# Where the Vector engine forms the quarter sums of the activations for the down projection

## The chip, the cores and the metric

The kernel runs on one core of a Trainium2 chip. The metric is the device time of one execution in microseconds (us); where several executions are compared, it is their median. TensorE (PE) multiplies matrices, VectorE (DVE) and ScalarE (ACT) work elementwise, GpSimd (POOL) helps, and SyncE (SP) issues most of the loads.

## What is computed

One layer of a decoder trunk, for a prompt of 512 tokens and 8 sample tokens, 520 in all. The change touches only its last part, the feed-forward block:

```python
    xn = rmsnorm(x, g2)
    up = xn @ w_up                                  # 1024 -> 2 * 2816
    pad = jnp.concatenate([conv_buf.astype(up.dtype), up], axis=1)
    conv = c_b + c_w[0] * pad[:, 0:S]
    for j in range(1, CONV_W):
        conv = conv + c_w[j] * pad[:, j:j + S]
    a, gval = jnp.split(conv, 2, axis=-1)
    x = x + (jax.nn.silu(a) * gval) @ w_down        # 2816 -> 1024
```

## The kernel before, in words

**Numbers in two parts.** Every f32 operand of a matmul is held as a high part in the reduced f32 format that TensorE takes (names in `h`, `whi`) and a low part, the rest (names in `l`, `wlo`). A product of two operands is three matmuls: high by high, high by low, low by high. ACT makes a high part by copying, DVE the low part by subtracting the high part from the original. Weights come by DMA into two buffers `raw_pair` (`raw[0]`, `raw[1]`), are split into `whi[0/1]` and `wlo[0/1]`, and slot n uses buffer n mod 2. A matmul takes 128 weight columns and 260 of the 520 tokens (`HALF`).

**Up projection.** It has 22 steps (`FT` = 22), i = 0 to 21, each of two tiles of 48 matmuls (t = 0 and 1). In step i DVE (`up_step`, L1629) scales a finished tile out of PSUM into `up[t]` (L1645), subtracts the low part of an earlier activation (`hidden_low`, L1622), makes `wlo` for the tile two slots on (`low`, L1083), runs the causal convolution (L1652 to L1656) and multiplies the two branches (L1660). The results are the activations `acth` (high) and `actl` (low), 22 blocks of 128 features by 520 tokens. Steps 1 to 17 are a hardware loop on DVE; steps 18 to 21 are written out.

**Down projection.** The 22 blocks of activations are cut into groups of 8, 7 and 7. There are 8 output tiles. For the first 6, taken as 3 pairs (`pairs_d`), the group of 8 blocks is done with a scheme of 7 products in place of 8 (`DownPair`, `down_pair`): a 2 by 2 block product, the quarters being 4 blocks by 260 tokens. It needs the activations' quarters as ordinary f32 sums and four combinations of them: with a quarter sum `acth + actl` called Q(k, h), k for the blocks (0 to 3 or 4 to 7) and h for the half of the tokens,

- act00 = Q(0,0), act01 = Q(0,1), act10 = Q(4,0), and dtf[1] = Q(4,1);
- combination 0 = act01 - act00, combination 2 = dtf[1] - combination 0, combination 1 = dtf[1] - act01, combination 3 = act10 - combination 2.

Each combination gets a high part `dth` (ACT) and a low part `dtl` (DVE, L1703). They are made once and serve all three pairs. Seven factors of each pair's weights are made likewise: DVE forms four sums `dsum` of weight blocks (L1709 to L1714), ACT their high parts, DVE their low parts (`factor_low`, L1491).

**The order around the change.** PE is one queue: after the last up tile it runs four slots of pair 0 (S_DN to S_DN + 3; 42 matmuls each, blocks 8 to 21), then products 0 to 6 of pair 0 (12 matmuls each), then pair 1, pair 2, a plain tile, and the last tile. A slot n begins when `w_lo` says that DVE's `low(n)` is done. Product f waits for `s_pl`, DVE's low part of factor f (`product`, L2175); product 3 waits besides for two low parts `dtl`, products 5 and 6 for the others (`s_tl`). DVE works in the order of its program too: three of the four quarter sums stand in steps 18, 19 and 20 (`extra=`, put between the two tiles of a step), the first combination in step 21; behind `hidden_low(21)` come, in this order, the fourth quarter sum, `low(S_DN+2)`, three subtractions that make the other combinations, `low(S_DN+3)`, four `dtl`, a memset, and pair 0's factors. ACT waits with `s_bt` for each combination in the order 0, 2, (high part of slot S_DN+3's weights), 1, 3, and only then makes the factors' high parts. SP issues the load into a raw buffer when the low part of its former contents is done.

Of the kernel before, what the change touches and what calls it, by code (L numbers as in the profile page):

```python
# [19 lines left out]
ALU = mybir.AluOpType  # L20
# [10 lines left out]
KT = D_MODEL // P  # L31
NC = SEQ // P
FT = D_FF // P
# [16 lines left out]
S_DN = S_UP + 2 * FT  # L50
# [36 lines left out]
def hybrid_layer(nc, ins, outs):  # L87
    with ExitStack() as ctx:
# [12 lines left out]
        def sem(name):  # L101
            return ctx.enter_context(nc.semaphore(name))
# [109 lines left out]
        def st(name, shape, offset):  # L212
            return nc.alloc_sbuf_tensor_at(name, shape, F32, offset=stage_at + offset)
# [20 lines left out]
        act00 = nc.alloc_sbuf_tensor_at("act00", [P, KT // 2, HALF], F32, offset=sp_at)  # L234
        act01 = nc.alloc_sbuf_tensor_at("act01", [P, KT // 2, HALF], F32, offset=ftmp_at)
        act10 = st("act10", [P, KT // 2, HALF], 0)
# [72 lines left out]
        def down_width(g):  # L309

            return (DN_CUTS[g + 1] - DN_CUTS[g]) * P
# [95 lines left out]
        s_bt = sem("x_combinations")  # L407
# [668 lines left out]
        def _(dve):  # L1076
            TT, TS, STT = dve.tensor_tensor, dve.tensor_scalar, dve.scalar_tensor_tensor

            def low(n, width=KT * P):

                p = n.c % 2
                dve.wait_ge(w_hi, n(1))
                TT(wlo[p][:, 0:width], raw[p][:, 0:width], whi[p][:, 0:width].bitcast(F32), ALU.subtract)\  # L1083
                    .then_inc(w_lo, 1)

            def ready(n):
                dve.wait_ge(done, n(2))

            def both(t):
                return t.rearrange("p (a b) -> p a b", a=2)  # L1090

            def out2(n):
                return out_ps[n.c % 2][:, :, 0:HALF]
# [525 lines left out]
            def hidden_low(i):  # L1619

                dve.wait_ge(s_ah, i + 1)
                TT(actl[:, i, :], silu[:, :], acth[:, i, :].bitcast(F32), ALU.subtract).then_inc(s_al, 1)  # L1622

            def quarter_sum(out, k0, h):

                part = (slice(None), slice(k0, k0 + KT // 2), slice(h * HALF, (h + 1) * HALF))
                TT(out, acth[part].bitcast(F32), actl[part].bitcast(F32), ALU.add)

            def up_step(i, first=False, last=False, extra=None):  # L1629
                for t in range(2):  # L1630
                    n = At(S_UP + t, i, 2)
                    f = i * 2 + t
                    if extra is not None and t == 1:
                        extra()
                    if first and t == 0:
                        dve.memset(up[0][:, 0:2], 0.0)
                        dve.memset(up[1][:, 0:2], 0.0)
                        dve.wait_ge(s_std2, 1)
                        dve.reciprocal(rbc2[:, :], rbc2[:, :])
                        low(n.plus(2))  # L1640
                        dve.drain()
                    ready(n)
                    if not first:
                        dve.wait_ge(s_nc, i * 2 + (t - 1))
                    TT(both(up[t][:, 2:2 + TOK]), out2(n), both(rbc2[:, :]), ALU.mult).then_inc(evac[n.c % 2], 1)  # L1645
                    dve.drain()  # L1646
                    dve.nop().then_inc(s_up, 1)
                    if t == 0 and not first:
                        hidden_low(i - 1)
                    if not (first and t == 0):  # L1650
                        low(n.plus(2), down_width(1 + t) if last else KT * P)
                    STT(conv[t][:, SEQ:TOK], up[t][:, 2 + SEQ:2 + TOK], cwb[:, f, 2:3], sconv[:, f, :], ALU.mult, ALU.add)  # L1652
                    dve.wait_ge(s_tap, i * 2 + (t + 1))
                    STT(conv[t][:, 0:SEQ], up[t][:, 1:1 + SEQ], cwb[:, f, 1:2], conv[t][:, 0:SEQ], ALU.mult, ALU.add)
                    dve.drain()
                    STT(conv[t][:, 0:SEQ], up[t][:, 0:SEQ], cwb[:, f, 0:1], conv[t][:, 0:SEQ], ALU.mult, ALU.add)\  # L1656
                        .then_inc(s_cv, 1)
                dve.drain()
                dve.wait_ge(s_sil, i + 1)
                TT(silu[:, :], silu[:, :], conv[1][:, :], ALU.mult).then_inc(s_pr, 1)  # L1660

            dve.wait_ge(s_scv, 1)
            up_step(0, True)
            with dve.Fori(1, FT - 4) as i:
                up_step(i)

            def first_difference():

                TT(act00[:, :, :], act01[:, :, :], act00[:, :, :], ALU.subtract).then_inc(s_bt, 1)

            up_step(FT - 4, extra=lambda: quarter_sum(act00[:, :, :], 0, 0))
            up_step(FT - 3, extra=lambda: quarter_sum(act01[:, :, :], 0, 1))
            up_step(FT - 2, extra=lambda: quarter_sum(act10[:, :, :], KT // 2, 0))
            up_step(FT - 1, last=True, extra=first_difference)
            hidden_low(FT - 1)

            def low_last():
# [78 lines left out]
                result()  # L1756

            dve.wait_ge(s_nc, 2 * FT)
            quarter_sum(dtf[:, 1, :, :], KT // 2, 1)
            low(At(S_DN + 2), down_width(1))  # L1760
            dve.drain()
            TT(dtf[:, 2, :, :], dtf[:, 1, :, :], act00[:, :, :], ALU.subtract).then_inc(s_bt, 1)
            TT(dtf[:, 1, :, :], dtf[:, 1, :, :], act01[:, :, :], ALU.subtract).then_inc(s_bt, 1)
# [685 lines left out]
```

## Time and profile before

| | us |
|---|---|
| median of 3 runs | 898.91 (898.21 to 899.29) |
| the profiled execution's own time | 898.24 |
| its span, first to last instruction | 896.4 |
| PE busy in the span | 887.7 (99%) |
| DVE busy | 609.7 (68%) |
| ACT busy | 390.5 (44%) |
| POOL busy | 133.0 (15%) |

The mean granted TensorE clock of the span is 0.997 of full speed. Busy shares are means over stages that differ. The last up tile ends near 765 us and pair 0 of the down projection lies between 765 and 795 us of the span; all times in the rows below are counted from the span's start. PE's rows overlap: the modelled duration of one matmul is 0.28 us, while one starts every 0.12 us, so the starts are what tells its pace. On DVE, too, an instruction may start a little before the row of the one ahead of it ends.

### The profile page before, as it was taken

What the parts mean: (1) busy time and instruction counts of PE and PEld (TensorE: products, weight loads), DVE (VectorE), ACT (ScalarE), POOL (GpSimd) and SP (SyncE); (2) the same over time, 40 slices, a digit from 0 to 9 for tenths busy, and PEclk for the clock granted to TensorE, in tenths of its full rate; (3) what the DMA queues carried; (4) which work ended last, traced back from release to release, by engine and by line L of the source; (5) the groups of instructions that cost most, each with busy time, mean ns of one, the idle gap of its engine ahead of it and who ended that gap; (6) DMA issues with size and microseconds to landing.
All of it is one profiled execution on the core that took longest, in us unless ns stands there. A gap on an engine that the chain in (4) does not pass through costs nothing.

```text
span 896.4 us, 18963 instructions
## 1 busy us (share of the span) xinstructions
PE 887.7 (99%) x7306; PEld 883.2 (99%) x7306; DVE 609.7 (68%) x980; ACT 390.5 (44%) x629; POOL 133.0 (15%) x182
## 2 busy tenths in 40 slices
PE   9999999999999999999999999999999999999997
PEld 8999999999999999999999999999999999999997
DVE  7895775442885568677755777777777778966544
ACT  7535434544864334344432344444444444433334
POOL 0673000002542110000005700000000000000001
PEclk9999999999999999999999999999999999999998
DMA  6332253234872222322255222222222222333232
GB/s 214 114 123 94 72 202 99 78 99 155 280 269 72 71 72 75 115 95 94 95 200 136 83 82 94 94 94 94 94 88 82 87 94 88 99 107 88 89 106 96
DMA packets 31499, 100.44 MB, mean 112 GB/s; under 512 B 4668, under 2 KB 7260, under 8 KB 31192
## 3 DMA queue, kind: packets, MB, share of 16 engines
q1 hardware_dynamic: 29256, 92.96, 31.2%
q0 software_dynamic: 1472, 5.72, 2.2%
q10 hardware_dynamic: 720, 1.04, 0.4%
q8 instruction: 36, 0.59, 0.3%
q14 instruction: 15, 0.12, 0.0%
HBM read 92.37 MB, written 7.35 MB: 111 GB/s over the span
## 4 chain that ended last, share of the span: by engine, by line
PE 88%; issue 3%; POOLq 3%; DMA 2%; DVE 2%; POOL 1%; ACT 0%; DVEq 0%; SPq 0%; ACTq 0%
PE out L1961 81%; PE trp L1961 3%; PE aux L1961 2%; POOLq L1939 2%; POOLq L1937 1%; DMA raw_pair<-in_w_slots 1%; PE trp L1995 1%; DMA cwb<-in_conv_wb 1%; PE aux L2153 0%; DVE wlo L1083 0%; DVE tf L1425 0%; DVE tl L1430 0%; POOL y L1952 0%; DVE tf L1421 0%; POOL out_conv_old L1923 0%
## 5 line engine op out<-in xcount | busy, mean ns | idle before, releaser
L581 ACT ACTIVATE whi<-raw_pair 128x1024 fp32r<-128x1024 f32 (+4 forms) x168 | 154.2, 924 | 210.3 <-PE out L1961 196.4
L1083 DVE TENSOR_TENSOR wlo<-raw_pair,whi 128x1024 fp32r<-128x1024 f32 (+1 forms) x121 | 154.0, 1273 | 89.6 <-ACT whi L581 89.2
L1961 PE MATMUL out<-xh,whi 128*128 128x260 f32 x668 | 143.4, 289 | 0.4 <-DVE wlo L1491 0.4
L1961 PE MATMUL out<-x2h,wlo 128*128 128x260 f32 x704 | 141.9, 283 | 0.0
L1961 PE MATMUL out<-x2h,whi 128*128 128x260 f32 x704 | 141.8, 282 | 0.0
L1961 PE MATMUL out<-x2l,whi 128*128 128x260 f32 x704 | 141.7, 283 | 0.0
L1961 PE MATMUL out<-xl,whi 128*128 128x260 f32 x668 | 139.3, 283 | 0.0
L1961 PE MATMUL out<-xh,wlo 128*128 128x260 f32 x668 | 139.2, 283 | 0.0
L1961 PEld LDWEIGHTS out<-x2h,whi 128*128 128x128 f32 x704 | 108.6, 188 | 0.1
L1961 PEld LDWEIGHTS out<-x2h,wlo 128*128 128x128 f32 x704 | 108.5, 188 | 0.0
L1961 PEld LDWEIGHTS out<-x2l,whi 128*128 128x128 f32 x704 | 108.2, 188 | 0.0
L1961 PEld LDWEIGHTS out<-xh,whi 128*128 128x128 f32 x668 | 105.4, 189 | 1.0 <-issue 0.6
L1961 PEld LDWEIGHTS out<-xh,wlo 128*128 128x128 f32 x668 | 105.0, 188 | 0.0
L1961 PEld LDWEIGHTS out<-xl,whi 128*128 128x128 f32 x668 | 104.9, 188 | 0.0
L1961 PE MATMUL out<-acth,whi 128*128 128x260 f32 (+2 forms) x266 | 58.2, 283 | 0.0
L1961 PE MATMUL out<-acth,wlo 128*128 128x260 f32 (+2 forms) x266 | 58.0, 283 | 0.0
L1961 PE MATMUL out<-actl,whi 128*128 128x260 f32 (+2 forms) x266 | 57.9, 283 | 0.0
L1645 DVE TENSOR_TENSOR up<-out,rbc 128x520 f32<-128x520 f32 x44 | 30.8, 701 | 38.9 <-PE out L1961 38.8
L1945 POOL COPY nconv<-up 128x10 f32 x44 | 10.4, 236 | 241.4 <-DVEq L1646 241.4
L581 ACT ACTIVATE acth<-silu 128x520 f32 (+1 forms) x22 | 14.1, 639 | 69.8 <-DVE silu L1660 69.8
L1961 PEld LDWEIGHTS out<-acth,whi 128*128 128x128 f32 x266 | 42.8, 188 | 0.1
L1961 PEld LDWEIGHTS out<-acth,wlo 128*128 128x128 f32 x266 | 42.8, 188 | 0.0
(362 smaller groups left out, 1755.8 us busy)
## 6 DMA issues: line engine op xcount, KB each, us to landing
raw_pair<-in_w_slots SPq DMA_DIRECT2D x123, 512.0 KB, 3.3
raw_pair<-in_w_dn SPq DMA_DIRECT2D x16, 448.0 KB, 3.4
c_ring<-in_C_state SPq DMA_DIRECT2D x8, 512.0 KB, 5.4
row<-scratch SPq DMA_DIRECT2D x8, 512.0 KB, 5.7
out_C_sample<-c_ring SPq DMA_DIRECT2D x8, 512.0 KB, 4.9
raw_pair<-in_w_dn SPq DMA_DIRECT2D x8, 512.0 KB, 3.5
xres<-in_x_all POOLq DMA_DIRECT2D x1, 1560.0 KB, 6.9
x<-in_x_all SPq DMA_DIRECT2D x5, 260.0 KB, 6.8
```

Of the source, the lines that this page charges most:

```text
L581: return act.activation(out, in_, func, **kw_)
L1083: TT(wlo[p][:, 0:width], raw[p][:, 0:width], whi[p][:, 0:width].bitcast(F32), ALU.subtract)\
L1645: TT(both(up[t][:, 2:2 + TOK]), out2(n), both(rbc2[:, :]), ALU.mult).then_inc(evac[n.c % 2], 1)
L1937: pool.drain()
L1939: pool.drain()
L1945: pool.tensor_copy(nconv[:, i * 2 + t, :], up[t][:, SEQ:2 + TOK]).then_inc(s_nc, 1)
L1961: return pe.matmul(*a, **k)
L1995: m = pe.transpose(trp[b.c % 2][:, c, :], ftmp[b.c % 2][:, c * P:(c + 1) * P], ident[:, :])
```

## The change

The three quarter sums in steps 18, 19 and 20 and the first combination in step 21 are taken out of the up projection. All four sums and all four combinations now stand behind `hidden_low(21)`. The steps 18 to 20 join the hardware loop. ACT, PE, SP and POOL keep their programs instruction for instruction; DVE runs the same operations on the same operands, four of them later.

```diff
             up_step(0, True)
-            with dve.Fori(1, FT - 4) as i:
+            with dve.Fori(1, FT - 1) as i:
                 up_step(i)
-
-            def first_difference():
-
-                TT(act00[:, :, :], act01[:, :, :], act00[:, :, :], ALU.subtract).then_inc(s_bt, 1)
-
-            up_step(FT - 4, extra=lambda: quarter_sum(act00[:, :, :], 0, 0))
-            up_step(FT - 3, extra=lambda: quarter_sum(act01[:, :, :], 0, 1))
-            up_step(FT - 2, extra=lambda: quarter_sum(act10[:, :, :], KT // 2, 0))
-            up_step(FT - 1, last=True, extra=first_difference)
+            up_step(FT - 1, last=True)
             hidden_low(FT - 1)
...
             dve.wait_ge(s_nc, 2 * FT)
+            quarter_sum(act00[:, :, :], 0, 0)
+            low(At(S_DN + 2), down_width(1))
+            quarter_sum(act01[:, :, :], 0, 1)
             quarter_sum(dtf[:, 1, :, :], KT // 2, 1)
-            low(At(S_DN + 2), down_width(1))
+            dve.drain()
+            TT(act00[:, :, :], act01[:, :, :], act00[:, :, :], ALU.subtract).then_inc(s_bt, 1)
+            quarter_sum(act10[:, :, :], KT // 2, 0)
             dve.drain()
             TT(dtf[:, 2, :, :], dtf[:, 1, :, :], act00[:, :, :], ALU.subtract).then_inc(s_bt, 1)
             TT(dtf[:, 1, :, :], dtf[:, 1, :, :], act01[:, :, :], ALU.subtract).then_inc(s_bt, 1)
```

In the rows below L1627 is the line of a quarter sum, L1083 that of `low`, and the number behind a name counts its buffer. On DVE, in step 21, between the convolution of the first tile and the scaling of the second, the row with the minus goes (one like it, an L1627, goes from each of steps 18 to 20):

```order
 L1654 SCALAR_TENSOR_TENSOR conv_84<-up_82,cwb,conv_84 128x512
 L1656 SCALAR_TENSOR_TENSOR conv_84<-up_82,cwb,conv_84 128x512
-L1669 TENSOR_TENSOR act_152<-act_153,act_152 128x1040
 L1645 TENSOR_TENSOR up_83<-out,rbc_87 128x520
 L1083 TENSOR_TENSOR wlo_123<-raw_pair,whi_121 128x896
```

The step's second tile now follows its first with nothing between them.

On DVE behind the last up step, before the change, from `hidden_low(21)` to the first `dtl`; `wlo1_124` is the low part of slot S_DN+2's weights, `wlo0_123` that of slot S_DN+3's:

```order
L1622 TENSOR_TENSOR actl_64<-silu_86,acth_119 128x520
L1627 TENSOR_TENSOR dtf_91<-acth_119,actl_64 128x1040
L1083 TENSOR_TENSOR wlo1_124<-raw_pair_120,whi1_122 128x896
L1762 TENSOR_TENSOR dtf_91<-dtf_91,act00_152 128x1040
L1763 TENSOR_TENSOR dtf_91<-dtf_91,act01_153 128x1040
L1765 TENSOR_TENSOR dtf_91<-act10_154,dtf_91 128x1040
L1083 TENSOR_TENSOR wlo0_123<-raw_pair_120,whi0_121 128x896
L1703 TENSOR_TENSOR dtl_90<-act00_152,dth_89 128x1040
```

The same place after the change (line numbers behind L1661 are 8 lower at first, 3 lower behind the edit):

```order
L1622 TENSOR_TENSOR actl_64<-silu_86,acth_119 128x520
L1627 TENSOR_TENSOR act00_152<-acth_119,actl_64 128x1040
L1083 TENSOR_TENSOR wlo1_124<-raw_pair_120,whi1_122 128x896
L1627 TENSOR_TENSOR act01_153<-acth_119,actl_64 128x1040
L1627 TENSOR_TENSOR dtf_91<-acth_119,actl_64 128x1040
L1756 TENSOR_TENSOR act00_152<-act01_153,act00_152 128x1040
L1627 TENSOR_TENSOR act10_154<-acth_119,actl_64 128x1040
L1759 TENSOR_TENSOR dtf_91<-dtf_91,act00_152 128x1040
L1760 TENSOR_TENSOR dtf_91<-dtf_91,act01_153 128x1040
L1762 TENSOR_TENSOR dtf_91<-act10_154,dtf_91 128x1040
L1083 TENSOR_TENSOR wlo0_123<-raw_pair_120,whi0_121 128x896
L1695 TENSOR_TENSOR dtl_90<-act00_152,dth_89 128x1040
```

`low(S_DN+2)` still has one instruction between it and `hidden_low`; between it and `low(S_DN+3)` there are seven in place of three.

## Rows read from the trace of the kernel before

**Rows 1.** The page, busy time and share of the span by engine.

```profile
PE 887.7 (99%) x7306; PEld 883.2 (99%) x7306; DVE 609.7 (68%) x980; ACT 390.5 (44%) x629; POOL 133.0 (15%) x182
```

**Rows 2.** Timeline, DVE, steps 17 to 19: start, duration, what, [idle before].

```profile
713.19 0.70 DVE L1645 TENSOR_TENSOR up<-out,rbc 128x520 f32<-128x520 f32 x1 [0.95 <-PE out L1961]
...
724.63 0.70 DVE L1645 TENSOR_TENSOR up<-out,rbc 128x520 f32<-128x520 f32 x1 [0.87 <-PE out L1961]
...
728.85 1.23 DVE L1627 TENSOR_TENSOR act<-acth,actl 128x1040 f32<-128x1040 f32 x1
730.40 0.70 DVE L1645 TENSOR_TENSOR up<-out,rbc 128x520 f32<-128x520 f32 x1 [0.32 <-PE out L1961]
...
736.16 0.70 DVE L1645 TENSOR_TENSOR up<-out,rbc 128x520 f32<-128x520 f32 x1 [1.03 <-PE out L1961]
```

**Rows 3.** Timeline, DVE, step 21 between its two tiles.

```profile
763.31 1.24 DVE L1669 TENSOR_TENSOR act<-act,act 128x1040 f32<-128x1040 f32 x1
765.00 0.70 DVE L1645 TENSOR_TENSOR up<-out,rbc 128x520 f32<-128x520 f32 x1 [0.45 <-PE out L1961]
```

**Rows 4.** Timeline, DVE, behind the last up step.

```profile
770.32 0.70 DVE L1622 TENSOR_TENSOR actl<-silu,acth 128x520 fp32r<-128x520 f32 x1 [0.76 <-ACT acth L581]
770.93 1.23 DVE L1627 TENSOR_TENSOR dtf<-acth,actl 128x1040 f32<-128x1040 f32 x1
772.09 1.08 DVE L1083 TENSOR_TENSOR wlo<-raw_pair,whi 128x896 fp32r<-128x896 f32 x1
773.26 1.24 DVE L1762 TENSOR_TENSOR dtf<-dtf,act 128x1040 f32<-128x1040 f32 x1
774.42 1.24 DVE L1763 TENSOR_TENSOR dtf<-dtf,act 128x1040 f32<-128x1040 f32 x1
775.75 1.24 DVE L1765 TENSOR_TENSOR dtf<-act,dtf 128x1040 f32<-128x1040 f32 x1
776.91 1.08 DVE L1083 TENSOR_TENSOR wlo<-raw_pair,whi 128x896 fp32r<-128x896 f32 x1
777.91 1.23 DVE L1703 TENSOR_TENSOR dtl<-act,dth 128x1040 fp32r<-128x1040 f32 x1
...
783.07 1.22 DVE L1491 TENSOR_TENSOR wlo<-raw_pair,whi 128x512 fp32r<-128x512 f32 x2
784.21 0.68 DVE L1709 TENSOR_TENSOR dsum<-raw_pair 128x512 f32<-128x512 f32 x1
...
787.16 2.52 DVE L1491 TENSOR_TENSOR wlo<-dsum,whi 128x512 fp32r<-128x512 f32 x4
```

**Rows 5.** Timeline, PE: starts of slot S_DN+3, product 0, product 1, product 2.

```profile
779.94 0.40 PE L1961 MATMUL out<-acth,whi 128*128 128x260 f32 x2
...
784.99 0.28 PE L1961 MATMUL trp<-acth,whi 128*128 128x260 f32 x1
...
786.41 0.28 PE L1961 MATMUL out<-acth,whi 128*128 128x260 f32 x1
...
787.73 0.28 PE L1961 MATMUL out<-acth,wlo 128*128 128x260 f32 x1
787.91 0.39 PE L1961 MATMUL out<-acth,whi 128*128 128x260 f32 x1
```

**Rows 6.** Timeline, ACT: combinations' high parts and slot S_DN+3's.

```profile
771.03 1.07 ACT L581 ACTIVATE dth<-act 128x1040 fp32r<-128x1040 f32 x1
774.54 1.08 ACT L581 ACTIVATE dth<-dtf 128x1040 fp32r<-128x1040 f32 x1 [2.44 <-DVE dtf L1762]
775.52 0.94 ACT L581 ACTIVATE whi<-raw_pair 128x896 fp32r<-128x896 f32 x1
776.36 2.02 ACT L581 ACTIVATE dth<-dtf 128x1040 fp32r<-128x1040 f32 x2
```

**Rows 7.** L471, the loads into the raw buffers, 740 to 800 us.

```profile
DMA to landing us min/median/max: 3.3/3.4/3.6
```

**Rows 8.** Waits of PE, 730 to 896 us: us in total, times, longest.

```profile
PE out L1961 <- ACT sqa L581: 0.6, 1, 0.6
PE aux L1961 <- DVE nd L1818: 0.6, 1, 0.6
```

**Rows 9.** Windows, PE, in the tail: us, busy (x), granted clock, DMA share, GB/s.

```profile
888.50:889.00 0.50, 0.01 (x1) 1.00 1.00 349
...
891.00:891.50 0.50, 0.41 (x4) 1.00 1.05 374
891.50:892.00 0.50, 0.00 (x0) 0.87 0.13 40
```

## The prediction

> **What bounds the kernel now.** I read the page's first part first: PE is busy 99% of the span and DVE 68% [rows 1]. That says only that PE must be kept fed; it doesn't say whether moving four DVE instructions is free. For that I took the two places between which they move, first on DVE's timeline, then on PE's.
>
> In the up projection PE sets the pace. The first tile of a step is scaled at 713.19, 724.63 and 736.16 us; the interval from step 18 (with a quarter sum) to step 19 is 11.53 us, and steps 17 to 18 (no sum) took 11.44, the loop's last step included. Each time DVE had waited for PE: 0.95 us in a step without a sum, and still 0.32 us right behind the quarter sum of 1.23 us [rows 2]. In step 21 the subtraction of 1.24 us is followed by 0.45 us of waiting [rows 3]. So before the change the four instructions lie wholly in time in which DVE would have waited.
>
> Behind the last up step it is the other way round. From 770.32 to 788 us DVE has no idle time in its rows but drains of a tenth [rows 4]. PE starts product 2 of pair 0 at 787.91, 0.18 us after the matmul ahead of it where the pace is 0.12; product 2 needs the low part of factor 2, the first of the four at 787.16, which ends near 787.16 + 0.69 = 787.85 [rows 4, 5]. So PE is already fed just in time there: DVE's chain has at most about 0.06 us to spare. From then until the last matmuls of the kernel PE waits for nobody: 0.6 and 0.6 us are all its waits of 730 to 896 us, both at the end, on the last squares and the last reciprocal [rows 8]. A delay at product 2 therefore has nowhere to vanish.
>
> **What is removed.** Steps 18 to 21 lose 1.23 or 1.24 us of DVE each. What comes next in each step is the scaling of a tile that PE has to finish first, so DVE's idle time there grows from 0.32 (0.45) to about 1.5 us and nothing starts earlier. Cost and gain 0. The steps 18 to 20 now run as loop passes; in the trace a looped and a written-out step both keep PE's interval, so 0 again.
>
> **What is added behind the last step.** DVE's start-to-start intervals: an instruction of 128x1040 with no drain behind it takes 770.93 to 772.09 = 1.16 us, and 773.26 to 774.42 = 1.16; `low` takes 776.91 to 777.91 = 1.00 us; with a drain behind it `low` takes 772.09 to 773.26 = 1.17 and the subtraction 774.42 to 775.75 = 1.33, so a drain costs 0.17 [rows 4]. Three quarter sums and one subtraction are added, and one drain: 4 x 1.16 + 0.17 = **4.81 us**. (The three new sums read the same operands in the same form as the old one, so its row prices them; bounds are 4 x 1.16 = 4.64 with a free drain and 4 x 1.24 + 0.17 = 5.13 without overlap.)
>
> The Trainium skill, in "VectorE: DVE Perf Modes", section "The DRAIN you can't avoid", says that the next operation doesn't issue until the pipeline is empty, whether or not a semaphore stands between. Taken literally that gives the upper of those bounds; the rows, with starts 1.16 us apart for a duration of 1.23, speak for the lower price.
>
> The new schedule, from 770.93: sum 00; `low(S_DN+2)` at 772.09, as before, so slot S_DN+2 is untouched; sum 01 at 773.09; sum 11 at 774.25; the first combination 775.58 to 776.82; sum 10 at 776.74; combinations 2, 1, 3 at 778.07, 779.23, 780.56; `low(S_DN+3)` at 781.72 in place of 776.91, ended 782.80.
>
> **What PE does with it.** Three waits open one after another, and together they make up the shift of DVE's chain:
> - Slot S_DN+3 started at 779.94 [rows 5]. It now waits for `low(S_DN+3)`, ended 782.80; with 0.06 us of signal it starts at 782.86: 2.92 us late.
> - It ran 779.94 to 784.99 = 5.05 us [rows 5], so it would end at 787.91. The factors' low parts come at 783.07 + 4.81 = 787.88; the first is done after half of 1.22 and a little overlap, 788.51. Product 0 starts at 788.57: 3.58 late, 0.66 more.
> - Products 0 and 1 take 787.91 - 784.99 = 2.92 us with the old gap, 2.86 without. Product 1's factor is done at 789.1, in time. Product 2 needs factor 2 at 787.85 + 4.81 = 792.66 and would be ready at 791.43: it starts at 792.72, 4.81 late in all, 1.23 more.
>
> Behind that DVE waited for ACT and PE before the change and waits again; the combinations' low parts are ready by 787.9, product 3 begins 1.5 us after product 2. So the shift stays 4.81.
>
> **Who else is shifted.** ACT waits with `s_bt` for the first combination: it ran at 771.03 and now starts at 776.86. Behind it in ACT's queue stand the second `dth` (DVE gives it at 779.31; 779.35 to 780.4) and the high part of slot S_DN+3's weights, which started 0.98 us after it [rows 6]: 780.33 to 781.27. DVE wants that at 781.72, so it is covered, by 0.45 us; were ACT late by more, `low(S_DN+3)` would move one for one. The two other `dth` end near 783.3 and DVE takes their low parts in its order 0, 2, 1, 3 from 782.72, the third at 785.0: covered. Two factors' high parts follow by 784.4, wanted at 787.88. SP's load for pair 0's second raw buffer waits for `low(S_DN+3)`: issued at 782.9, landed 3.4 us later [rows 7], 786.3; its first reader, the weight sum of 784.21, now comes at 789.0 [rows 4]. Covered by 2.7 us. SP's following loads wait for the weight sums and move with DVE, keeping their margins.
>
> **The forecast.** The profiled execution took 898.24 us (span 896.4), which gives 898.24 + 4.81 = 903.05. The median of the runs is 0.67 above that execution, and the sum moves with it: 898.91 + 4.81 = 903.72. I take 903.7, 0.5% slower; about 0.2% (1.8 us) is what a measurement of this kernel can tell from no change.
>
> **Rivals.**
> - **Only the first wait counts** (901.8). If the waits at products 0 and 2 had more slack than the rows say, PE would lose 2.92 us only. Against it: the gap of 0.18 us at 787.91 and the factor's end at 787.85 [rows 4, 5]. Chance 5%.
> - **The clock falls in the new wait.** The granted clock stayed 1.00 through half a microsecond with PE at 0.01, and fell to 0.87 in the window at 891.5, after about 3 us of thin work in the tail [rows 9]. A stall of 2.92 us is near that. If the clock were at its lower level, 1.2 GHz in place of 2.4, for all of slot S_DN+3, that slot would take 5.05 us more; but 0.66 + 1.23 = 1.89 us of it would fall into waits that exist anyway. That leaves 3.2 us: 906.9. Half such a spell costs 0.6 us. Chance of any such fall 12%; only half of that costs over 1.8 us.
> - **A pause at DVE's loop end.** The loop ends at step 20 now, next to the exposed stretch. In the trace the loop's end at step 17 leaves 0.87 us of waiting for PE [rows 2], so any pause there is hidden. The Trainium skill, "Runtime: NRT & Kernel Launch", section "Instruction fetch mechanics", says a taken branch whose target lies outside the fetched blocks stalls the engine for a transfer. As a mechanism here: a pause as long as a load's landing, 3.4 us [rows 7], less the 0.87 to 1.5 us in which DVE waits, lets PE run dry or moves the chain by some 2.2 us: 905.9. Chance 4%.
> - **The other side: the up projection gets faster** (not slower in all). The removed sums read and write SBUF beside PE's operands. If they had held PE up, steps 18 to 21 would shorten, and from 1.2 us a step on (4.81 / 4) the change would not lose. But a step with a sum takes 11.53 us and one without 11.44: at most 0.09 a step, 0.4 in all, 903.3. That the sum decides otherwise has 3%, and the same bucket holds any slack I have overlooked downstream.
>
> **How the numbers follow.** Forecast 76%, first wait only 5%, clock 12%, loop end 4%, other side 3%. The forecast itself reaches from 4.64 to 5.13, with half a microsecond either way for the medians: 903.0 to 904.6. To hold 8 in 10 against the rivals, the range goes from the first-wait case, 901.8, to 905.6, short of the full clock case. Faster by over 0.2% gets 2%, within 0.2% gets 3% (the other side and slack overlooked), slower 95%.
>
> **What would show it.** Right: in steps 18 to 21 DVE waits about 1.5 us before the second tile's scaling and PE's interval stays 11.53; `low(S_DN+3)` starts 9.6 us behind `low(S_DN+2)` in place of 4.8; PE shows waits on `wlo` L1083 of 2.6 to 2.9 us and twice on L1491, of 0.7 and 1.2, with the granted clock at 1.00; everything behind 793 us is 4.8 later. Wrong: shorter up steps, no wait at product 2, a clock below 1.00 near 783, or an ACT wait in front of `low(S_DN+3)`.

## The result, and the profile after

The changed kernel takes 903.50 us (median of 5 runs, 902.65 to 904.09), the kernel before 898.91 (5 runs, 898.21 to 899.29): a ratio of 1.0055, 95% interval 1.0043 to 1.0066, and the medians differ by 4.6 us where 4.8 was forecast. The profiled execution took 902.65 us with a span of 900.8 (898.24 and 896.4 before).

The page says almost nothing of it: PE's busy share is the same 99% [rows 1].

```profile
PE 889.7 (99%) x7306; PEld 884.9 (98%) x7306; DVE 611.1 (68%) x980; ACT 390.6 (43%) x629; POOL 130.7 (15%) x182
```

PE's waits over the whole span say more (engine, line, whom it waited for: us in total, times, longest). Two of its rows are new where the kernel before had no wait between 730 us and the tail [rows 8]:

```profile
PE out L1958 <- DVE wlo L1083: 2.7, 1, 2.7
...
PE out L1958 <- DVE wlo L1491: 0.2, 1, 0.2
```

DVE's timeline of the changed kernel, at steps 15 and 19 to 21 first (answering [rows 2, 3]), then behind the last step (answering [rows 4]). L1756 is the first combination:

```profile
689.80 0.70 DVE L1645 TENSOR_TENSOR up<-out,rbc 128x520 f32<-128x520 f32 x1 [0.95 <-PE out L1958]
...
741.61 0.70 DVE L1645 TENSOR_TENSOR up<-out,rbc 128x520 f32<-128x520 f32 x1 [1.15 <-PE out L1958]
...
747.46 0.70 DVE L1645 TENSOR_TENSOR up<-out,rbc 128x520 f32<-128x520 f32 x1 [0.96 <-PE out L1958]
...
753.14 0.70 DVE L1645 TENSOR_TENSOR up<-out,rbc 128x520 f32<-128x520 f32 x1 [1.15 <-PE out L1958]
...
758.91 0.70 DVE L1645 TENSOR_TENSOR up<-out,rbc 128x520 f32<-128x520 f32 x1 [0.87 <-PE out L1958]
...
764.67 0.70 DVE L1645 TENSOR_TENSOR up<-out,rbc 128x520 f32<-128x520 f32 x1 [1.60 <-PE out L1958]
...
771.76 1.08 DVE L1083 TENSOR_TENSOR wlo<-raw_pair,whi 128x896 fp32r<-128x896 f32 x1
772.76 1.23 DVE L1627 TENSOR_TENSOR act<-acth,actl 128x1040 f32<-128x1040 f32 x1
773.92 1.23 DVE L1627 TENSOR_TENSOR dtf<-acth,actl 128x1040 f32<-128x1040 f32 x1
775.23 1.24 DVE L1756 TENSOR_TENSOR act<-act,act 128x1040 f32<-128x1040 f32 x1
776.38 1.23 DVE L1627 TENSOR_TENSOR act<-acth,actl 128x1040 f32<-128x1040 f32 x1
...
781.34 1.08 DVE L1083 TENSOR_TENSOR wlo<-raw_pair,whi 128x896 fp32r<-128x896 f32 x1
```

Step 21's scaling now waits 1.60 us for PE where it waited 0.45, and starts no earlier in the step: 764.67 - 758.91 = 5.76 us behind the first tile's, 5.77 before (765.00 - 759.23). The steps 18 to 20, now loop passes, keep PE's interval too: from second tile to second tile 741.61, 753.14 and 764.67, so 11.53 us, as before from 730.40 to 765.00, three steps [rows 2, 3]. The two `low` start 9.58 us apart (4.82 before).

PE's timeline at the same place, answering [rows 5]; the last three rows are the start of product 0, the last matmul of product 1 and the start of product 2:

```profile
779.38 0.40 PE L1958 MATMUL out<-acth,wlo 128*128 128x260 f32 x2
782.48 0.50 PE L1958 MATMUL out<-acth,whi 128*128 128x260 f32 x2 [2.70 <-DVE wlo L1083]
782.83 0.51 PE L1958 MATMUL out<-actl,whi 128*128 128x260 f32 x2
783.13 0.64 PE L1958 MATMUL out<-acth,wlo 128*128 128x260 f32 x2
...
789.12 0.29 PE L1958 MATMUL trp<-acth,whi 128*128 128x260 f32 x1
...
791.89 0.28 PE L1958 MATMUL out<-acth,wlo 128*128 128x260 f32 x1
792.34 0.39 PE L1958 MATMUL out<-acth,whi 128*128 128x260 f32 x1 [0.17 <-DVE wlo L1491]
```

and the granted clock there (window, us, busy (x), granted clock as a share of 2.4 GHz, DMA share, GB/s):

```profile
782.00:783.00 1.00, 0.52 (x4) 0.98 0.00 0
783.00:784.00 1.00, 1.00 (x7) 0.50 0.62 98
784.00:785.00 1.00, 1.00 (x6) 0.50 0.89 344
785.00:786.00 1.00, 1.00 (x7) 0.50 0.21 82
786.00:787.00 1.00, 1.00 (x9) 0.82 0.00 0
787.00:788.00 1.00, 1.00 (x11) 1.00 0.00 0
```

Two things are seen. Product 2 starts 792.34 - 771.76 = 20.58 us behind `low(S_DN+2)`, 787.91 - 772.09 = 15.82 before: 4.76 us later. And the clock did fall: for about 3.4 us behind the wait it stood at its lower level of 1.2 GHz, and slot S_DN+3 took 789.12 - 782.48 = 6.64 us in place of 5.05. That rival had been given 12%, yet the time is that of the forecast. The experiments had to tell whether the 4.6 us are DVE's chain, with the clock's 1.59 us hidden, or the first wait and the clock together, 2.9 + 1.6, which gives nearly the same sum.

Counting from `low(S_DN+2)` is needed because executions differ by some tenths of a microsecond (once by 1.3) in what lies ahead: in the changed kernel's profile that instruction starts 0.33 us earlier than in the one before. The edited steps did not bring that: step 15, ahead of all that was edited, is already 0.32 us earlier (689.80 in the changed kernel). Its row in the kernel before:

```profile
690.12 0.70 DVE L1645 TENSOR_TENSOR up<-out,rbc 128x520 f32<-128x520 f32 x1 [0.95 <-PE out L1961]
```

4.76 - 0.33 = 4.43, and the two spans differ by 4.4.

### The profile page after: what moved, and what is told of

It reads as the page before. It is cut to its first block, busy times and chain, and to the rows that moved or that the text cites. A ratio compares the mean times of both kernels' runs of the same rounds, so it can differ in the third digit from the quotient of the medians.

```text
span 900.8 us, 19015 instructions
## 1 busy us (share of the span) xinstructions
PE 889.7 (99%) x7306; PEld 884.9 (98%) x7306; DVE 611.1 (68%) x980; ACT 390.6 (43%) x629; POOL 130.7 (15%) x182
## 4 chain that ended last, share of the span: by engine, by line
PE 88%; POOLq 3%; issue 3%; DVE 2%; DMA 1%; POOL 1%; ACT 1%; DVEq 1%; SPq 0%; ACTq 0%
PE out L1958 81%; PE trp L1958 3%; PE aux L1958 2%; POOLq L1936 2%; POOLq L1934 1%; PE trp L1992 1%; DMA cwb<-in_conv_wb 1%; DMA raw_pair<-in_w_slots 0%; DVE dtl L1695 0%; PE aux L2150 0%; POOL y L1949 0%; DVE act L1627 0%; DVE wlo L1083 0%; ACT whi L581 0%; POOL out_conv_old L1920 0%
## 5 line engine op out<-in xcount | busy, mean ns | idle before, releaser
L1083 DVE TENSOR_TENSOR wlo<-raw_pair,whi 128x1024 fp32r<-128x1024 f32 (+1 forms) x121 | 156.3, 1292 | 87.4 <-ACT whi L581 87.0
```

## Experiments

Times are medians; each group of kernels ran with the kernel before on its own chip (898.84 us for the first four, 898.20 for the next four, 898.55 for the last two). Beside its runs above, the changed kernel ran in the first group only. "Chain" is the theory that product 2 of pair 0 is late by as much as DVE's chain is longer.

**One, two and three late.** The first takes one instruction out of the up steps, the second two, the third three of the four:

```diff
-            up_step(FT - 2, extra=lambda: quarter_sum(act10[:, :, :], KT // 2, 0))
+            up_step(FT - 2)
...
             low(At(S_DN + 2), down_width(1))
+            quarter_sum(act10[:, :, :], KT // 2, 0)
             dve.drain()
```

> The kernel before, with one of the four moved instructions: the sum act10 is taken out of step 20 and stands behind low(S_DN+2). Theory of the chain (every late instruction delays product 2 of pair 0 by its start-to-start interval, 1.16 us, less 0.05 of slack): 1.1 us slower than before, near 900.0, PE waiting 1.1 us at product 2 and nowhere else, granted clock 1.00. Theory of the first wait and the clock (the loss is slot S_DN+3's wait, which has 1.95 us of slack in the kernel before, plus what the half-speed clock behind it takes): no change, 898.9.

> The kernel before, with two of the four moved: the sum act10 and the first combination act01 - act00 stand behind low(S_DN+2). Chain: 2 x 1.16 - 0.05 = 2.3 us slower, near 901.2, a wait of 0.4 us at slot S_DN+3 and 1.9 in all before product 2, clock 1.00. First wait and clock: 0.4 us slower, 899.3.

> The changed kernel with one sum left where it was: act00 in step 18; the sums act01 and act10 and the first combination are late, steps 18 to 20 written out. Chain: 3 x 1.16 + 0.17 - 0.05 = 3.6 us slower than before, near 902.5, slot S_DN+3 waiting about 1.7 us, too short for the clock to fall. First wait and clock: 1.7 us slower, 900.6.

> The changed kernel as it is, beside the three partial ones on the same chip. Both theories are built on it: 4.6 to 4.8 us slower than before, near 903.6. If the loss were not additive, the four kernels would not stand 1.1 to 1.3 us apart from each other.

Measured, with the places read from the four traces (the times of `low(S_DN+2)` and product 2 are starts in each kernel's own trace):

| late | median us | ratio to before, 95% | `low(S_DN+2)` | product 2 | between | more than before |
|---|---|---|---|---|---|---|
| 0 (before) | 898.84 | | 772.09 | 787.91 | 15.82 | |
| 1 | 899.18 | 1.0009 (1.0000 to 1.0018) | 771.65 | 788.60 | 16.95 | 1.13 |
| 2 | 901.21 | 1.0027 (1.0017 to 1.0037) | 772.50 | 790.60 | 18.10 | 2.28 |
| 3 | 902.46 | 1.0042 (1.0029 to 1.0056) | 771.52 | 790.94 | 19.42 | 3.60 |
| 4 (changed kernel again) | 903.61 | 1.0062 (1.0048 to 1.0076) | 771.88 | 792.46 | 20.58 | 4.76 |

The traces give a straight line: 1.13, 1.15, 1.32 (the one with the drain) and 1.16 us for the four. The theory of first wait and clock wanted 0, 0.4, 1.7 and 4.6; the medians of two (2.4 us) and three (3.6 us) late are far from its 0.4 and 1.7. For one late the median difference of 0.3 us alone can't decide; its interval (0 to 1.6 us) holds both. The spans of all executions, from first to last instruction, tell them apart better: their medians are 896.6 us before and 897.3, 898.9, 900.0 and 901.3 with one to four late, so 0.7, 2.3, 3.4 and 4.7 more. All 11 spans with one late are 897.0 us or longer, 16 of the 19 before are shorter, and the trace shows the new wait of 0.99 us at product 2. So one late does cost time. In the profiled executions the 0.7 us of span (897.1 against 896.4) are the 1.13 less the 0.44 by which `low(S_DN+2)` came earlier; the others have no trace. With two late, PE's three waits of the prediction stand side by side for the first time, with the clock at 1.00 throughout:

```profile
PE out L1963 <- DVE wlo L1491: 1.0, 1, 1.0
PE trp L1963 <- DVE wlo L1491: 0.4, 1, 0.4
PE out L1963 <- DVE wlo L1083: 0.2, 1, 0.2
```

A wait in these rows begins at the modelled end of the last matmul. By starts, one matmul every 0.12 us, each is 0.16 to 0.3 longer. Three late, where the first is 1.55 us, also left the clock alone:

```profile
781.08 0.51 PE L1960 MATMUL out<-acth,whi 128*128 128x260 f32 x2 [1.55 <-DVE wlo L1083]
...
786.78 0.39 PE L1960 MATMUL trp<-acth,whi 128*128 128x260 f32 x1 [0.39 <-DVE wlo L1491]
...
790.94 0.39 PE L1960 MATMUL out<-acth,whi 128*128 128x260 f32 x1 [1.02 <-DVE wlo L1491]
```

Here slot S_DN+3 at full clock would end at 781.08 + 5.05 = 786.13, and product 0 starts at 786.78: 0.65 late (the prediction had 0.66). Product 2 is 790.94 - 786.78 - 2.86 = 1.30 late (1.23).

**PE kept busy in the wait.** 22 matmuls whose result nobody reads:

```diff
                 for s in range(4):
                     t, g = s // 2, 1 + s % 2
                     if g == 1:
                         pe.wait_ge(evac[banks[t]], At(S_DN + pr.j + t).half(1))
+                    if pr.i == 0 and s == 3:
+                        for _ in range(22):
+                            MM(pr.p1, acth[:, 0, 0:P], acth[:, 0, 0:HALF], start=True, stop=True)
                     down_slot(...)
```

> The changed kernel, with 22 matmuls of 128x260 that nobody reads put on PE between slots S_DN+2 and S_DN+3 of pair 0, inside the wait of 2.7 us; they write the bank that product 0 overwrites. They should keep the granted clock at 1.00. Chain: the half-speed spell costs nothing, because PE waits at product 2 for DVE anyway; time unchanged at 903.5, and the 1.7 us that slot S_DN+3 gains turn into waits at products 0 and 2 (0.7 and 1.2 us, as the prediction had them). Clock: 1.7 us faster than the changed kernel, 901.8.

903.31 us, ratio 1.0056 (1.0042 to 1.0070). The clock stays up, here in the windows that had 0.50 in the changed kernel:

```profile
783.00:784.00 1.00, 1.00 (x11) 1.00 0.77 106
784.00:785.00 1.00, 1.00 (x11) 1.00 0.91 369
785.00:786.00 1.00, 1.00 (x10) 1.00 0.20 66
```

and what it gains comes back as waits, while product 2 starts as late as ever (792.19 - 771.61 = 20.58 us behind `low(S_DN+2)`, to the hundredth that of the changed kernel):

```profile
788.03 0.39 PE L1958 MATMUL trp<-acth,whi 128*128 128x260 f32 x1 [0.39 <-DVE wlo L1491]
...
792.19 0.39 PE L1958 MATMUL out<-acth,whi 128*128 128x260 f32 x1 [1.00 <-DVE wlo L1491]
```

So the fall of the clock costs nothing in the changed kernel: it takes 1.59 us, and 0.65 + 1.30 = 1.95 us of waiting stood behind it. The remainder, 0.36 us, is seen as the late start of product 2 behind product 1 in the changed kernel's trace (789.12 + 2.86 = 791.98 to 792.34).

**The sums done twice.** The steps stay as in the kernel before, and all four instructions are done again behind the last step (the edit is shown against the kernel before):

```diff
             def first_difference():
 
-                TT(act00[:, :, :], act01[:, :, :], act00[:, :, :], ALU.subtract).then_inc(s_bt, 1)
+                TT(act00[:, :, :], act01[:, :, :], act00[:, :, :], ALU.subtract)
...
             dve.wait_ge(s_nc, 2 * FT)
+            quarter_sum(act00[:, :, :], 0, 0)
+            low(At(S_DN + 2), down_width(1))
+            quarter_sum(act01[:, :, :], 0, 1)
             quarter_sum(dtf[:, 1, :, :], KT // 2, 1)
...
```

> The kernel before with its three sums and the first combination in steps 18 to 21 as they were, steps written out, and all of them done a second time behind the last step, in the order of the changed kernel. Chain: what stands in the up projection costs nothing and removing it earned nothing, so the same time as the changed kernel, 903.5, within 0.2. If the removal had earned something in steps 18 to 21 (0.09 us a step at most by the rows), or the loop's end had cost something, this kernel would differ from the changed one: up to 0.4 slower by the first, faster by the second.

903.30 us, ratio 1.0059 (1.0045 to 1.0072); product 2 at 792.39 - 771.81 = 20.58 us, the same as in the changed kernel. The two other kernels of its group in which DVE's way to product 2 is as long (below and above) take 903.42 and 903.31. The removal from the up steps earned nothing that can be seen, and loop or written-out steps make no difference.

**Slot S_DN+3 first.** On ACT the high part of that slot's weights goes ahead of the first combination's, on DVE its low part directly behind the first combination:

```diff
             TT(act00[:, :, :], act01[:, :, :], act00[:, :, :], ALU.subtract).then_inc(s_bt, 1)
+            low(At(S_DN + 3), down_width(2))
             quarter_sum(act10[:, :, :], KT // 2, 0)
...
-            low(At(S_DN + 3), down_width(2))
             down_combination_low(0, act00[:, :, :], 1)
```

> The changed kernel, but slot S_DN+3's weights are served early: ACT makes their high part before the first combination's, DVE their low part right behind the first combination, four instructions earlier. Nothing is added or left out. Chain: slot S_DN+3 starts on time, but product 2 is as late as in the changed kernel, the waits before products 0 and 2 add up to the same 4.7 us; 903.5, or up to 1.6 more if the longer wait before product 0 (3.6 us) lets the clock fall while products 0 and 1 run and only 1.2 us of that is hidden. First wait: the loss goes with the wait, 899 to 900.

903.42 us, ratio 1.0057 (1.0043 to 1.0070). The wait of 2.7 us is gone and the time is the same. Most of the debt now stands before product 0, which starts 788.41 - 771.99 = 16.42 us behind `low(S_DN+2)`, 784.99 - 772.09 = 12.90 in the kernel before, so 3.52 us later:

```profile
784.63 0.41 PE L1958 MATMUL out<-acth,wlo 128*128 128x260 f32 x2
788.41 0.39 PE L1958 MATMUL trp<-acth,whi 128*128 128x260 f32 x1 [3.36 <-DVE wlo L1491]
...
789.60 0.42 PE L1958 MATMUL trp<-acth,whi 128*128 128x260 f32 x1
789.82 0.42 PE L1958 MATMUL trp<-actl,whi 128*128 128x260 f32 x1
...
794.36 0.28 PE L1958 MATMUL trp<-dth,whi 128*128 128x260 f32 x1
```

The clock fell here too, 1.1 us after the wait, when products 0 and 1 ran (a start every 0.22 us from 789.60 to 792.85). That slowness fills the 1.24 us that are left before product 2, and a little more. Product 3 starts 794.36 - 771.99 = 22.37 us behind `low(S_DN+2)`, 793.87 - 771.76 = 22.11 in the changed kernel: 0.26 us is what was not hidden. It's too little to be seen in the medians.

**In the order in which PE needs it.** Everything stays late, but the four `dtl` (4.6 us on the path to product 2) move behind the factors 0 to 3, each ahead of the product that reads it, and slot S_DN+3's weights are served early. In short (ACT's high parts, not shown, follow the same order: slot S_DN+3's behind the first combination's, those of combinations 1 and 3 behind the factors 0 and 1):

```diff
             TT(act00[:, :, :], act01[:, :, :], act00[:, :, :], ALU.subtract).then_inc(s_bt, 1)
+            low(At(S_DN + 3), down_width(2))
             quarter_sum(act10[:, :, :], KT // 2, 0)
...
-            low(At(S_DN + 3), down_width(2))
-            down_combination_low(0, act00[:, :, :], 1)
-            down_combination_low(2, dtf[:, 2, :, :], 2)
-            down_combination_low(1, dtf[:, 1, :, :], 3)
-            down_combination_low(3, dtf[:, 3, :, :], 4)
...
                 factor_low(pr, 3)
+                if mixed:
+                    down_combination_low(2, dtf[:, 2, :, :], 2)
+                    down_combination_low(0, act00[:, :, :], 2)
                 factor_low(pr, 4)
+                if mixed:
+                    down_combination_low(1, dtf[:, 1, :, :], 3)
                 factor_low(pr, 5)
+                if mixed:
+                    down_combination_low(3, dtf[:, 3, :, :], 4)
+                    factor_low(pr, 6)
...
-                pe.wait_ge(s_tl, 4 + 2)
+                pe.wait_ge(s_tl, 4 + 1)
                 product(pr, 3, pr.p6, *down_combination(2)).then_inc(s_pd, 1)
+                pe.wait_ge(s_tl, 4 + 2)
```

> The changed kernel with everything late, but DVE (and ACT with it) takes its work in the order in which PE needs it: slot S_DN+3's weights behind the first combination, then the combinations, then pair 0's factors 0 to 3, and only then the four low parts of the combinations, each beside the product that reads it; product 3 no longer waits for combination 0. Chain: the work is the same, but four low parts (4.6 us) leave the path to product 2, product 2 would be about 0.6 late, and the last combination makes product 6 late by 1.5 to 2; 900.4 to 901.5, so 2 to 3 us of the loss come back. If it were the amount of late work and not its order that counts: 903.5.

902.41 us, ratio 1.0044 (1.0030 to 1.0057): only 1 us back, less than expected. Its trace names the reason, an idle spell of DVE in the middle of the chain:

```profile
776.85 1.24 DVE L1766 TENSOR_TENSOR act<-act,act 128x1040 f32<-128x1040 f32 x1
780.13 1.09 DVE L1084 TENSOR_TENSOR wlo<-raw_pair,whi 128x896 fp32r<-128x896 f32 x1 [2.04 <-ACT whi L581]
```

In this kernel ACT still made the first combination's high part before slot S_DN+3's. It could begin that only when DVE had formed the combination, and DVE, now due for `low(S_DN+3)` right behind it, had to wait for both. The next kernel swaps the two on ACT:

```diff
+            split(At(S_DN + 3), down_width(2))
             down_combination_hi(0, act00[:, :, :], 1)
-            split(At(S_DN + 3), down_width(2))
             down_combination_hi(2, dtf[:, 2, :, :], 2)
```

> The kernel in deadline order, but ACT makes the high part of slot S_DN+3's weights before the first combination's, so that DVE doesn't wait 2.04 us for it ahead of low(S_DN+3). From the trace of the deadline kernel, counted from low(S_DN+2): product 2 would come at 17.61 - 2.0 = 15.6 us (15.82 in the kernel before, so on time), DVE's last low part before pair 1's first slot ends at 26.7 - 2.0 = 24.7 where PE wants it at 23.1: 1.5 us late. Chain: 1.5 us slower than before, 2.0 faster than the first deadline kernel, 3.2 faster than the changed kernel. If DVE's wait for ACT was not on the path: no faster than the first deadline kernel.

900.30 us, ratio 1.0018 (1.0009 to 1.0027): by the medians 1.75 us slower than the kernel before on its chip (898.55), where the changed kernel was 4.6 and 4.8 us slower on its own, so some 3 us are back with the same late work. Of PE's waits in pair 0 one is left, at pair 1's first slot:

```profile
796.83 0.49 PE L1964 MATMUL out<-acth,whi 128*128 128x260 f32 x2 [0.39 <-DVE wlo L1737]
```

It starts 796.83 - 772.17 = 24.66 us behind `low(S_DN+2)`. In the kernel before, product 6 ends 795.21 - 772.09 = 23.12 behind it, in the changed one 799.63 - 771.76 = 27.87: late by 1.54 and 4.75, so by the traces 3.2 us of the 4.75 are back.

**The covered side, doubled.** The kernel before with each sum of steps 18 to 20 done twice in its place:

```diff
+            def twice(*a):
+                quarter_sum(*a)
+                dve.drain()
+                quarter_sum(*a)
...
-            up_step(FT - 4, extra=lambda: quarter_sum(act00[:, :, :], 0, 0))
-            up_step(FT - 3, extra=lambda: quarter_sum(act01[:, :, :], 0, 1))
-            up_step(FT - 2, extra=lambda: quarter_sum(act10[:, :, :], KT // 2, 0))
+            up_step(FT - 4, extra=lambda: twice(act00[:, :, :], 0, 0))
+            up_step(FT - 3, extra=lambda: twice(act01[:, :, :], 0, 1))
+            up_step(FT - 2, extra=lambda: twice(act10[:, :, :], KT // 2, 0))
```

> The kernel before, with each of the sums in steps 18, 19 and 20 done twice in a row in its place (a drain between; the second writes the same values): 1.33 us more of DVE work in each step where only 0.32 us of waiting is left ahead of the next scaling. Chain: the scaling comes about 1 us late in those steps, PE still finds its bank free because it runs a whole tile (5.76 us) in between, DVE has caught up at the end of the step, time unchanged, 898.9. If the remaining 0.32 us were all the cover there is: 3 x 1.0 = 3 us slower.

898.59 us, ratio 1.0000 (0.9991 to 1.0009). The scaling is late in the step and DVE has caught up by the next one:

```profile
728.92 2.55 DVE L1627 TENSOR_TENSOR act<-acth,actl 128x1040 f32<-128x1040 f32 x2
731.39 0.69 DVE L1645 TENSOR_TENSOR up<-out,rbc 128x520 f32<-128x520 f32 x1
...
736.23 0.70 DVE L1645 TENSOR_TENSOR up<-out,rbc 128x520 f32<-128x520 f32 x1 [0.37 <-PE out L1966]
```

PE's only wait from 700 to 890 us is one of 0.6 us, in the tail as before. So a microsecond of DVE work costs nothing in a step even beyond the 0.32 us of waiting that the kernel before shows there, and nearly all of itself behind the last step.

## Why the prediction was right, and where its picture was not

- **Nothing to gain in steps 18 to 21.** Right. PE's interval stays, and the kernel that did the sums twice is as slow as the changed one. Two readings on the way were off. The 11.44 us of steps 17 to 18 are no shorter step: they go from a loop pass to a written-out one, and the changed kernel has the same between steps 20 and 21, where its loop ends (758.91 - 747.46 = 11.45), so the 0.09 us a step of the last rival were no price of a sum. And DVE's wait grew to the forecast 1.5 us only in step 21 (1.60); in a loop pass it is 1.15 (at 753.14), because DVE starts its first tile 0.09 us later there and is 0.24 us slower from it to the end of the convolution (747.46 to 751.99 us, in the kernel before 747.70 to 751.99).
- **Three new sums, a subtraction and a drain, 4.81 us.** Measured 4.76: 1.16 for an instruction without a drain, as predicted, and 0.15 to 0.16 for the added drain where 0.17 was taken (773.92 to 775.23 is 1.31). The bound of 5.13 without overlap is ruled out: the instructions start 0.07 us before the row of the one ahead ends, here as in [rows 4]. The sentence of the Trainium skill that the prediction cites ("VectorE: DVE Perf Modes", section "The DRAIN you can't avoid") would give that bound if it stood alone; the same section adds that a next operation that is not held starts earlier, and the 0.07 us agree with that.
- **No slack at product 2 before the change.** Right: with one late, DVE's way from `low(S_DN+2)` to the low part of factor 2 is 787.85 - 771.65 = 16.20 us in place of 787.16 - 772.09 = 15.07, 1.13 longer, and product 2 is late by all of it.
- **Three waits of 2.92, 0.66 and 1.23 us.** The debt was right and its division only so without the fall of the clock. The kernel with three late shows 0.65 and 1.30 for the second and third; in the changed kernel slot S_DN+3's slow spell fills 1.59 us of them and 0.36 is left, so of the two waits on L1491 that the prediction named as its sign only one showed.
- **The clock keeps its level.** Wrong: it fell in both profiles of the changed kernel, which is one of the signs that the prediction itself had named for being wrong (a clock below 1.00 near 783). The prediction gave it 12% and its most probable course left it out. What saved the time was the step in the rival that set the clock's loss against the waits behind it; that step had 1.89 us of such waits, 1.95 were there, and the loss was 1.59. With the kernel that kept PE busy this is shown, not only argued. That the spell was short enough is luck: the prediction had no row for its length. It lasted about 3.4 us and cost 1.59; over the whole slot it would have cost 5.05 by the prediction's own sum, 3.1 more than the waits could take.
- **ACT, SP and the loads covered.** Right for the changed kernel: ACT's high part of slot S_DN+3 ran from 779.95 to 780.88, wanted at 781.34, a margin of 0.46 (0.45 predicted). How near ACT is to binding, the first deadline kernel showed, where DVE wanted that high part earlier and waited 2.04 us.
- **No pause at the loop's end.** Right: step 21's first scaling waits 0.87 us for PE at 758.91, as the first written-out step did in [rows 2]. The Trainium skill ("Runtime: NRT & Kernel Launch", section "Instruction fetch mechanics") warns of a stall at a taken branch whose target isn't in the fetched pages. No run here shows one.
- **903.7 us.** 903.5 measured. The sum was right for its own reasons, DVE's chain; the picture of PE beside it was not, in the one place named.

## What to carry to other kernels

Where an engine with a low busy share stands in a queue, price a moved instruction by the place, not by the share: the same 1.16 us cost nothing in a step that ends in a wait for PE, and nearly all of itself in a chain whose last link arrives when PE wants it. Several waits behind one long chain are one debt: curing the first only moves it to the next, and a slower clock inside it is free as long as it costs less than the waits behind it. If the work must be late, order it by who needs it first, on every engine it passes through; that brought back some 3 of 4.6 us without removing an instruction.

## What the runs showed of the chip

The granted clock fell to the lower of its two levels at single waits of PE: after 2.70 us of idle time in the changed kernel (both profiles) and 2.71 in the one with the sums done twice, and after 3.36 us in the one with slot S_DN+3 first; not after 1.55 us (three late), and not when unread matmuls filled the wait. These are one profile of each kernel, two of the changed one. Each time PE was already working again when the clock dropped, 0.2 to 1.4 us past its restart. In the profile shown above the level was low from about 783.0 to 786.4 us. In the kernel with the sums done twice it began latest:

```profile
783.00:784.00 1.00, 1.00 (x11) 0.95 0.54 74
784.00:785.00 1.00, 1.00 (x7) 0.50 0.81 319
785.00:786.00 1.00, 1.00 (x7) 0.50 0.33 131
786.00:787.00 1.00, 1.00 (x6) 0.50 0.00 0
```

In this place the wait of 2.7 us brought it about in three profiles of three, but probably not in every execution. A spell of 3.4 us at half the clock takes 0.0019 off the mean granted clock of an execution. The kernel before, without it, has 0.996 to 0.998, the changed kernel 0.994 to 0.996 in all ten executions; the kernel with the sums done twice has 0.998 in two of its five, and with the spell it would come out near 0.996 at best (0.998 - 0.0019). Those two took 903.35 and 903.30 us, the three others 903.08, 903.21 and 904.66: the two without the spell, by this reckoning, were not faster. It is worked out from means, since these two executions have no trace.
